# Gated one-hot rows of a two-layer decoder's expert gates: GpSimd subtracts, VectorE compares and gates four tokens in one operation

## The reference

```python
sv, si = lax.top_k(s, K)                         # per head: 16 best of 128 rows, 16 best of 128 columns
best, pos = lax.top_k(cand, K)                   # the 16 best pairs
eidx = jnp.take_along_axis(cidx, pos, axis=-1)   # expert = row * 128 + column
gate = jax.nn.softmax(best, axis=-1)
a = einsum('chkd,cd->chk', expert_u[ec], xc)     # each picked expert's input product
w = gc * gelu(a)
y = einsum('chk,chkd->cd', w, expert_v[ec])
x = layer_norm(ALPHA * x + y)
```

## Time and profile before

| | |
|---|---|
| median of 3 runs | 2398.19 us (2396.39 to 2401.14) |
| profiled execution | 2390.59 us, its span 2389.0 us |
| PE busy | 2192.5 us (92%) |
| DVE busy | 1578.3 us (66%) |
| ACT busy | 1186.3 us (50%) |
| POOL busy | 30.9 us (1%), 48 instructions |
| gate stage, both layers | about 119.3 and 119.1 us, 718.84 to 838.1 and 1903.2 to 2022.3 us |

### The profile page before, as it was taken

How to read it: one execution, slowest core, us unless ns; L and a number is a source line. 1 busy time by engine, 2 the same in 40 slices (tenths; PEclk the granted TensorE clock), 3 DMA queues, 4 the chain that set the end, 5 groups by cost and what they waited for, 6 DMA issues and landing times. The chain is left out here.

```text
span 2389.0 us, 43579 instructions
## 1 busy us (share of the span) xinstructions
PE 2192.5 (92%) x14072; PEld 1976.6 (83%) x14072; DVE 1578.3 (66%) x3274; ACT 1186.3 (50%) x2058; POOL 30.9 (1%) x48
## 2 busy tenths in 40 slices
PE   6989889999996699999989898999999867999997
PEld 6877779999995578788777867999999855887886
DVE  5646657777779955555557456477777798555555
ACT  4435444455457645455434344455445575554553
POOL 1000000000000000000000000000000000000000
PEclk9979999999998999999989899999999999999999
DMA  4612435555550045555546114355555400555554
GB/s 143 230 61 71 134 125 183 184 181 181 183 185 0 0 165 192 197 193 193 171 140 212 62 54 159 133 181 181 183 184 179 155 0 9 194 193 202 193 193 141
DMA packets 96305, 353.41 MB, mean 148 GB/s; under 512 B 11056, under 2 KB 11088, under 8 KB 95856
## 3 DMA queue, kind: packets, MB, share of 16 engines
q1 hardware_dynamic: 94032, 341.90, 42.5%
q0 software_dynamic: 2208, 10.66, 1.3%
HBM read 351.47 MB, written 1.05 MB: 148 GB/s over the span
## 5 line engine op out<-in xcount | busy, mean ns | idle before, releaser
L700 DVE TENSOR_TENSOR lo<-raw,hi 128x1024 fp32r<-128x1024 f32 x648 | 792.6, 1224 | 589.2 <-ACT hi L443 583.7
L443 ACT ACTIVATE hi<-raw 128x1024 fp32r<-128x1024 f32 x648 | 686.8, 1060 | 518.7 <-DMA raw<-in_peer_v 355.4
L1198 PE MATMUL acc<-xT_hi,lo 128*128 128x256 f32 x2560 | 733.7, 287 | 9.7 <-DVE xT_lo L778 7.2
L1199 PE MATMUL acc<-xT_lo,hi 128*128 128x256 f32 x2560 | 731.5, 286 | 0.0
L1200 PE MATMUL acc<-xT_hi,hi 128*128 128x256 f32 x2560 | 731.3, 286 | 0.0
L1198 PEld LDWEIGHTS acc<-xT_hi,lo 128*128 128x128 f32 x2560 | 499.3, 195 | 13.3 <-issue 11.4
L1199 PEld LDWEIGHTS acc<-xT_lo,hi 128*128 128x128 f32 x2560 | 499.0, 195 | 0.1
L1200 PEld LDWEIGHTS acc<-xT_hi,hi 128*128 128x128 f32 x2560 | 498.6, 195 | 0.0
L1209 PE MATMUL wide<-hi,w_lo 128*128 128x512 f32 x1024 | 318.9, 393 | 11.9 <-DVE w_lo L1157 11.9
L1209 PE MATMUL wide<-hi,w_hi 128*128 128x512 f32 x1024 | 317.3, 391 | 0.0
L1209 PE MATMUL wide<-lo,w_hi 128*128 128x512 f32 x1024 | 317.3, 391 | 0.0
(11 more groups left out here) (233 smaller groups left out, 1721.0 us busy)
## 6 DMA issues: line engine op xcount, KB each, us to landing
raw<-in_peer_u SPq DMA_DIRECT2D x256, 512.0 KB, 3.2
raw<-in_peer_v SPq DMA_DIRECT2D x256, 512.0 KB, 3.2
raw<-in_front SPq DMA_DIRECT2D x136, 512.0 KB, 3.3
ln_par<-in_ln POOLq DMA_DIRECT2D x10, 512.0 KB, 5.3
w<-in_cmp_w POOLq DMA_DIRECT2D x2, 2048.0 KB, 9.6
xs<-in_x SPq DMA_DIRECT2D x2, 512.0 KB, 6.8
keys<-in_sub_keys POOLq DMA_DIRECT2D x2, 512.0 KB, 3.5
out<-xs SPq DMA_DIRECT2D x1, 1024.0 KB, 3.9
```

Source lines behind the costliest of these rows:

```text
L443: nc.scalar.activation(hi[:, s], raw[:, s], ACT.Identity).then_inc(hi_done, 1)
L700: nc.vector.tensor_tensor(lo[:, s], raw[:, s], hi[:, s].bitcast(F32), ALU.subtract).then_inc(lo_done, 1)
L1198: mm(dst, lo[:, s, c], xh[:, k], start=k == 0, stop=False)
L1199: mm(dst, hi[:, s, c], xl[:, k], start=False, stop=False)
```

## The change

Three edits, all in the gate stage.

1. GpSimd gets a loop over the 64 groups of a layer. For each it waits until TensorE has finished the group four before, and writes `hot_j = iota - column` for four tokens in one TENSOR_TENSOR of 128 x 512. It begins when the first part of `picksT` is there, and each of its operations adds one to a new semaphore, `apart_j_ready`.
2. VectorE's `gated_rows` waits for that semaphore in place of `acc_ready`, and does `(hot_j == 0) * gate` in place, for four tokens in one SCALAR_TENSOR_TENSOR of 128 x 512, in place of four TENSOR_SCALARs of 128 x 128.
3. VectorE's `one_hot` does one TENSOR_TENSOR of 128 x 512 in place of four TENSOR_SCALARs.

```diff
+                pool.wait_ge(tr_read[X_PK % 2], OPEN + l * (NTR // 2) + NTR // 2)
+                pool.sem_inc(apart, 1)
+                with pool.Fori(0, NG // HOTS) as i:
+                    for e in range(HOTS):
+                        pool.wait_ge(acc_ready, l * NREADY + (R_G + 1 - HOTS) + (i * HOTS + e))
+                        toks = picksT[:, 1, bass.ds(i * (4 * HOTS) + 4 * e, 4)].unsqueeze(2).broadcast_to([P, 4, P])
+                        nc.gpsimd.tensor_tensor(hot_j[:, e], iota[:].unsqueeze(1).broadcast_to([P, 4, P]), toks,
+                                                ALU.subtract).then_inc(apart_j_ready, 1)
...
                 def gated_rows(i, e):
-                    dve.wait_ge(acc_ready, l * NREADY + (R_G + 1 - HOTS) + (i * HOTS + e))
-                    for r in range(4):
-                        tok = i * (4 * HOTS) + (4 * e + r)
-                        ins = nc.vector.tensor_scalar(hot_j[:, e % HOTS, r], iota[:], picksT[:, 1, bass.ds(tok, 1)],
-                                                      picksT[:, 2, bass.ds(tok, 1)], ALU.is_equal, ALU.mult)
-                    ins.then_inc(hot_j_ready, 1)
+                    dve.wait_ge(apart_j_ready, l * NG + (i * HOTS + (e + 1)))
+                    toks = picksT[:, 2, bass.ds(i * (4 * HOTS) + 4 * e, 4)].unsqueeze(2).broadcast_to([P, 4, P])
+                    nc.vector.scalar_tensor_tensor(out=hot_j[:, e % HOTS], in0=hot_j[:, e % HOTS], scalar=0.0, in1=toks,
+                                                   op0=ALU.is_equal, op1=ALU.mult).then_inc(hot_j_ready, 1)
...
                 def one_hot(i, e):
-                    for r in range(4):
-                        tok = i * (4 * HOTS) + (4 * e + r)
-                        ins = nc.vector.tensor_scalar(hot_i[:, e % HOTS, r], iota[:], picksT[:, 0, bass.ds(tok, 1)], None,
-                                                      ALU.is_equal)
-                    ins.then_inc(hot_i_odd, 1)
+                    toks = picksT[:, 0, bass.ds(i * (4 * HOTS) + 4 * e, 4)].unsqueeze(2).broadcast_to([P, 4, P])
+                    nc.vector.tensor_tensor(hot_i[:, e % HOTS], iota[:].unsqueeze(1).broadcast_to([P, 4, P]), toks,
+                                            ALU.is_equal).then_inc(hot_i_odd, 1)
```

More of the change, by code:

```diff
@@ L337, in build @@
         hot_i_odd = sem("hot_i_odd")
+        apart_j_ready = sem("apart_j_ready")
         hot_j_ready = sem("hot_j_ready")
```

## The result

The changed kernel takes 2400.46 us, median of 20 runs (2393.40 to 2407.22), against 2396.16 us for 20 runs of the kernel before (2390.19 to 2401.14): a ratio of 1.0021, 95% interval 1.0013 to 1.0029. It is 4.3 us slower. The direction was forecast; the size was not, since +20 us was. The time lies inside rival B's band as well (2394 to 2402 us).

A forecast was written before the change was run, and what follows sets the result against it. VectorE was taken to bound the gate stage (117.84 of 119.26 us busy). Iterations of 7.97 against 7.27 us gave +22, the stage's start -2: +20 on 2398.19, so 2418 us (+0.8%), 8-in-10 range 2350 to 2442.

The forecast's parts named there:

- rival B: Gate stage: both engines wait, but the subtraction is short, 0.93 us; iteration 7.29 us, 2394 to 2402 us; chance 0.10.
- VectorE's own work: Gate stage: VectorE's shorter gated rows and comparisons make an iteration 5.69 us, 1.58 less than 7.27.
- rival A: Gate stage: GpSimd is held, VectorE is not; iteration 5.69 us, about 2349 to 2358 us; chance 0.30.
- The subtraction: GpSimd's two-input operation of 128 x 512 in the gate stage: 1.10 us, bounds 0.87 to 1.29.
- Held both ways: Gate stage: GpSimd reading SBUF and VectorE operations with two SBUF inputs wait for each other; iteration 7.97 us.
- C: Gate stage: `gate_gelu` wants the port too; iteration 10.7 us, about 2500 us; chance 0.06.
- For the whole of an operation: Shared SBUF port: whichever of VectorE and GpSimd starts first makes the other wait until its operation ends.
- the row at 10.49: An `xs` operation on VectorE, started inside GpSimd's 10.26 to 10.82, that ran its usual 1.28 us.
- the sum of one group: Gate stage: gated rows, subtraction less 0.14 already behind it, and GpSimd-to-VectorE gap, one after the other: 1.82 us.
- GpSimd's buffers: Gate stage: GpSimd's wait for the group four before, 7.3 us back, costs 0.
- The start of the stage: Before the first gated rows: four subtractions done ahead, less holds of `lo` splits and L1105: -1 us a layer.
- theory L: Gate stage: the forecast's mutual holding of VectorE and GpSimd, sharpened in the experiments: what counts is when GpSimd starts.

The follow-up runs named there:

- edit 3 alone: Kernel before with only the fourth group's `hot_i` comparisons made one VectorE TENSOR_TENSOR of 128 x 512: 2389.65 against 2394.82 us.
- no subtraction: Changed kernel without GpSimd's subtractions, VectorE's gated rows reading `iota` instead: 2349.48 us against 2394.82 us for the kernel before.
- write only: Changed kernel with a GpSimd MEMSET of 128 x 512 in place of each subtraction, same waits: 2347.00 us against 2394.82 us for the kernel before.
- two of four: Changed kernel, GpSimd subtracting only for groups 1 and 3 of each four: 2367.67 against 2394.16 us before; with groups 0 and 2, 2379.93 against 2394.06.
- paced: Changed kernel, each GpSimd subtraction also waiting for the gated rows of the group two before: 2397.80 us against 2394.16 us for the kernel before.
- three of four: Changed kernel, GpSimd subtracting only for groups 1, 2 and 3 of each four: 2397.17 us against 2394.06 us for the kernel before.
- one of four: Changed kernel, GpSimd subtracting only for group 3 of each four: 2392.05 us against 2394.06 us for the kernel before.

## Why the prediction was right and wrong

- **VectorE's own work** was priced at 5.69 us an iteration and is 5.40: an operation of 128 x 512 takes 0.68 us, and the next starts after 0.60, for both new forms. I had taken the gated rows' 0.75 and 0.67 from `xs` (1024 elements), whose scalar is per partition; the new rows have a constant there and cost no more than a TENSOR_TENSOR. That the scalar makes the difference is a guess; no run shows it. Without the subtraction an iteration came to 5.73 because VectorE then waits for TensorE, and TensorE for ScalarE, at times. So two errors cancelled in rival A's 5.69, and its -49 to -40 us is what was measured where nothing holds VectorE, -45.
- **The subtraction** was taken as 1.10 us, and is 1.04 us alone; right within its bounds. At 1.04 the forecast's own sum would have been 7.73 an iteration.
- **Held both ways: right.** The changed kernel's rows show both directions, and three runs (edit 3 alone, no subtraction, write only) exclude that the operations are long by themselves or that the semaphore is what costs. Rivals A and C fell. Rival B's number came true (2394 to 2402 us) without its condition, a subtraction of 0.93 us. "For the whole of an operation" holds for the subtractions, not for every GpSimd record: the row at 10.49, which I had set aside because a transfer could explain its start, was a true sign. In four runs a `lo` split started 0.24 to 0.71 us after the start of GpSimd's four-element `rstd` operation of 1.04 us, and still took its usual 1.22 to 1.23. In two of four:

```profile
1230.94 1.04 POOL L410 TENSOR_TENSOR rstd<-var,neg_half 128x4 f32<-128x4 f32 x1 [38.10 <-DVE gsum L831]
1231.24 1.23 DVE L711 TENSOR_TENSOR lo<-raw,hi 128x1024 fp32r<-128x1024 f32 x1 [0.39 <-ACT hi L454]
```

- **The step that failed is the sum of one group,** "0.75 + 1.10 - 0.14 + 0.11 = 1.82 us". Its parts are mis-sized: 0.75 + 0.11 for a VectorE operation behind a GpSimd one is really 0.55. A held operation has its start behind it on both sides; I had seen that for GpSimd (0.14) and not granted it to VectorE, and the 0.11 is the price of a semaphore, which nobody was waiting for. Of the 0.31 that is too much, 0.07 is the operation's own length (0.75 for 0.68), 0.13 the start behind it, and 0.11 the semaphore. With 0.55 + 0.90 the group is 1.45, and an iteration 4 x 1.45 + 0.55 = 6.35 us, if one operation always follows on the other.
- **And a second error went the other way.** "GpSimd's buffers: it needs the group four before, 7.3 us back. 0." It is not 0. GpSimd sat idle for TensorE before 87 of its 128 subtractions, 74.8 us in all, so it is not always queued when VectorE lets go, and comes in ahead of VectorE at other times. 6.35 became a mean of 7.28 and 7.41. That this wait is the whole of the 1.0 is argued, not shown: no run gave GpSimd more buffers. My 7.97 erred by +1.6 and, on a mean of 7.34, by -1.0.
- **The start of the stage** was put at -1 us a layer and is +1: from L1098 to the first rows it is 7.75 us (715.73 to 723.48) against 6.75, since a `lo` split was held (2.06 us in place of 1.22), and a second one behind the first rows too. I had foreseen these holds and set the four subtractions done ahead against them; the iterations show no gain from those.
- **The `ln_par` loads and ScalarE** show no cost, as said. TensorE was put at nothing too, and VectorE waited for it before `gate_gelu` for 3.2 us in all, 0 before: little, but nearly as much as the 3.7 us that the two stages grew by.
- **Slips in the forecast's numbers.** "This case alone spans 2389 to 2442" became "2395 to 2442" without a reason. VectorE's busy time in the stage, "some 97 us", is 103 by its own records (64 x (0.75 + 0.68) + 16 x 0.69); it was 116 to 118, as held time counts as busy.

That the forecast's sign came out right was luck. The loss to the holds, 1.94 us an iteration (7.34 - 5.40), is just about the 1.87 us (7.27 - 5.40) that the change saves VectorE, and both of the errors above were larger than the difference. The same subtractions in another rhythm moved the time by 12 us, so a sign this close to zero was not to be had from the sum.

The kernels with 0, 1, 2 (two orders), 3 and 4 subtractions of four make it plain that their number does not predict the time: -5, -2, -27 or -14, +3, and +4 us for four.

## What to carry to other kernels

Work given to GpSimd is not free because GpSimd is idle: if it reads SBUF, it and VectorE's operations on SBUF stop each other, and the loss is in VectorE's durations, where no wait shows. Price the port as one shared resource, and then ask at which moment the helper is issued: with the start of a long VectorE operation it costs almost nothing, ahead of one or between short ones it costs most of its length (0.7 to 0.8 of 1.04 us here). Which it will be was hard to foresee: theory L's forecasts for paced, two of four, three of four and one of four all missed. So try the placements and read the timeline. Giving GpSimd half of the groups, so placed, made this kernel 1.2% faster, where all of them made it 0.2% slower.

## What the runs showed of the hardware

- VectorE and GpSimd's subtraction of 128 x 512 hold each other, both ways. A held 128 x 512 VectorE operation ended 0.55 us after GpSimd's end (0.68 us alone), a held subtraction 0.90 us after VectorE's (1.04 us alone). GpSimd's `rstd` operation of 128 x 4, also 1.04 us, was held (1.94 us) but held nothing: a `lo` split that started 0.30 us into it took 1.23 us.
- The order of two starts in the trace doesn't settle who has the port: with GpSimd's start recorded 0.04 us ahead (788.37 and 788.41) VectorE still went first, and so each time in that run; at 0.17 us ahead (773.65 and 773.82) GpSimd did, but in the changed kernel it also did at 0.03 us ahead (731.54 and 731.57, gated rows 1.56 us). What decides between starts this close no run shows.
- A VectorE TENSOR_SCALAR of 128 x 128 with one SBUF input is held as well, up to 1.11 us in place of 0.28, and ends 0.08 us after GpSimd's end; the TENSOR_TENSOR with one input in PSUM was not held (at most 0.69 us in 128, before and after).
- A GpSimd MEMSET of 128 x 512 (0.53 us) held nothing and was not held.
